# A single-core transformer pair of blocks: the opening's loads, squares and VectorE order rewritten, and TensorE's order in the banded attention

## What is computed

```python
h = _rmsnorm(x, norm_mix_g)
proj = h @ w_in                                   # short conv, long conv, queries, gates
memn = _rmsnorm(mem, norm_mem_g)
k, vm = jnp.split(memn @ w_kv, 2, axis=-1)        # 256 memory positions
...
merged = g[:, :, 0] * y_a + g[:, :, 1] * y_b + g[:, :, 2] * y_c
x = x + merged @ w_o
x = x + _conv_ffn(x, norm_ffn_g, w_up, conv_ffn_w, w_down)
...
q, k, v, z = jnp.split(xn @ w_in, [nq, nq + nkv, nq + 2 * nkv], axis=-1)
o = banded_attention(q, k, v, t5_table, SWA_WINDOW, sinks)
x = x + (o * jax.nn.silu(z)) @ w_out              # then a last RMS norm
```

## Time and profile before

| | before |
|---|---|
| median of 3 runs | 1213.76 us (1213.65 to 1213.79) |
| the profiled execution, its time | 1213.99 us |
| its span | 1212.2 us |
| granted TensorE clock, mean | 0.999 |
| PE busy | 1203.6 us, 99% |
| PE weight loads | 994.2 us, 82% |
| DVE busy | 827.7 us, 68% |
| ACT busy | 490.6 us, 40% |
| DMA over the span | 105 GB/s |

### The profile page before, as it was taken

How to read it: one execution, slowest core, us unless ns; L and a number is a source line. 1 busy time by engine, 2 the same in 40 slices (tenths; PEclk the granted TensorE clock), 3 DMA queues, 4 the chain that set the end, 5 groups by cost and what they waited for, 6 DMA issues and landing times.

```text
span 1212.2 us, 15930 instructions
## 1 busy us (share of the span) xinstructions
PE 1203.6 (99%) x5656; PEld 994.2 (82%) x5656; DVE 827.7 (68%) x1293; ACT 490.6 (40%) x785; POOL 7.5 (1%) x18
## 2 busy tenths in 40 slices
PE   9999999999999999999999999999999999999998
PEld 8788888888888888888888888888888888887786
DVE  6858897797789987554357866566654444578762
ACT  7543323332333323552334534334333333155643
POOL 0000000000000000000000000000000000000000
PEclk9999999999999999999999999999999999999999
DMA  8533232222222332243322232233233534221221
GB/s 325 175 104 104 87 104 73 84 87 86 71 87 87 104 105 87 87 174 104 104 78 97 87 106 90 98 104 104 87 110 104 174 104 139 87 71 53 74 66 70
DMA packets 35842, 125.51 MB, mean 104 GB/s; under 512 B 4081, under 2 KB 5761, under 8 KB 35537
## 3 DMA queue, kind: packets, MB, share of 16 engines
q1 hardware_dynamic: 33424, 116.41, 28.8%
q0 software_dynamic: 928, 6.08, 1.4%
q10 hardware_dynamic: 1440, 2.36, 0.5%
HBM read 122.72 MB, written 4.21 MB: 105 GB/s over the span
## 4 chain that ended last, share of the span: by engine, by line
PE 95%; DVE 2%; DMA 1%; ACT 0%; issue 0%; SPq 0%; DVEq 0%; ACTq 0%
PE acc L852 80%; PE acc L869 5%; PE side L1189 2%; PE acc L1189 2%; DMA w_raw<-weights 1%; PE side L1115 1%; PE acc L1153 1%; DVE w_low L1223 1%; PE acc L886 1%; PE side L991 1%; PE side L1011 1%; PE acc L1125 1%; DVE part L1260 0%; PE side L1001 0%; DVE part L1351 0%
## 5 line engine op out<-in xcount | busy, mean ns | idle before, releaser
L852 PE MATMUL acc<-h_high,w_high 128*128 128x512 f32 x880 | 343.2, 390 | 0.0
L852 PE MATMUL acc<-h_low,w_high 128*128 128x512 f32 x880 | 342.7, 389 | 0.0
L852 PE MATMUL acc<-h_high,w_low 128*128 128x512 f32 x880 | 342.7, 389 | 0.0
L1223 DVE TENSOR_TENSOR w_low<-w_raw,w_high 128x1024 fp32r<-128x1024 f32 x213 | 257.6, 1221 | 42.0 <-ACT w_high L474 38.8
L474 ACT ACTIVATE w_high<-w_raw 128x1024 fp32r<-128x1024 f32 x213 | 221.0, 1051 | 103.2 <-PE acc L852 86.9
L852 PEld LDWEIGHTS acc<-h_high,w_low 128*128 128x128 f32 x880 | 165.2, 188 | 34.3
L852 PEld LDWEIGHTS acc<-h_high,w_high 128*128 128x128 f32 x880 | 165.2, 188 | 34.3 <-DVE w_low L1223 0.2
L852 PEld LDWEIGHTS acc<-h_low,w_high 128*128 128x128 f32 x880 | 165.3, 188 | 33.9
L1298 DVE SCALAR_TENSOR_TENSOR convs<-long_u,par,convs 128x510 f32<-128x510 f32 (+28 forms) x232 | 170.3, 734 | 6.6
L852 PE MATMUL acc<-f_high,w_high 128*128 128x512 f32 x176 | 68.6, 390 | 0.0
L852 PE MATMUL acc<-f_low,w_high 128*128 128x512 f32 x176 | 68.5, 389 | 0.0
(11 more groups left out here) (331 smaller groups left out, 1815.5 us busy)
## 6 DMA issues: line engine op xcount, KB each, us to landing
w_raw<-weights SPq DMA_DIRECT2D x213, 512.0 KB, 3.3
x_in<-x SPq DMA_DIRECT2D x4, 512.0 KB, 10.1
x<-x POOLq DMA_DIRECT2D x1, 2048.0 KB, 8.7
rows_dram<-strip_dram POOLq DMA_DIRECT2D x1, 2048.0 KB, 11.3
w_raw<-weights SPq DMA_DIRECT2D x4, 384.0 KB, 7.0
mem_in<-mem ACTq DMA_DIRECT2D x4, 256.0 KB, 7.1
bias<-rows_dram POOLq DMA_DIRECT2D x1, 1024.0 KB, 7.1
out<-result ACTq DMA_DIRECT2D x4, 256.0 KB, 2.6
```

Source lines behind the costliest of these rows:

```text
L852: mm = pe.matmul(acc[:, bank, 0:width], w[:, s, (skip + b) * P:(skip + b + 1) * P], moving[v][:, k, :], start=first and b == 0 and w is w_ ...
L1223: dve.tensor_tensor(w_low[:, s, :], raw[s][:, :], w_high[:, s, :].bitcast(F32), ALU.subtract)\
```

## The change

**Loads of the opening.** The first piece of unit 0 and tile 0 of the memory are transfers of their own (128 KB each, semaphores `alone_landed` and `mem_alone_landed`), and the first piece of units 1 and 2 follows as a transfer of 256 KB. The memory's tile 1 is loaded by ACT, tiles 2 and 3 by the software queue of GpSimd (POOL), tiles 4 to 7 by SP. The parameters (`par`, 254 KB) move from ACT's queue to the end of SP's opening. ACT issues two transfers instead of six. Units 4 and 5 are loaded at once into two spare buffers (`w_spare`), ahead of x; `raw_of` picks them.

**Order of the pieces.** ACT and DVE do unit 0's piece, then the two tiles of the memory, then the pieces of units 1 and 2. PE takes a unit's two tiles before the next unit's, and waits for that unit's piece alone. The zero products are three instead of four. DVE waits for the gains before its first instruction.

**Squares.** One `tensor_reduce` sums the memory's eight tiles (2048 elements a partition), one more those of x (4096 elements), both reading along k with n outside, so that neighbours in the sum lie 1 KB and 2 KB apart. They replace three additions of 128x512 and one of 128x256, and seven of 128x512.

**Order of DVE, ACT and PE** between unit 3 and unit 17: as in the diff; `total(N_X)` moves behind `value_slab(0, 0)`, `spread(N_X)` behind `value_slab(0, 1)`, tiles 5, 6 and 7 of x behind unit 17.

**Banded attention.** `outputs(j)` no longer follows `product` of its own iteration, but the two turns of the next one.

```diff
@@ sync
-            for c in range(CHUNKS):
+            def first_piece(c, u):
                 at = c * CHUNK
+            sp.dma_start(w_raw[:, 0, 0:CHUNK], weights[0, :, 0:CHUNK]).then_inc(alone_landed, 16)
+            sp.dma_start(mem_in[:, 0, :], mem[:, 0, :]).then_inc(mem_alone_landed, 16)
+            first_piece(0, 1)
+            first_piece(1, 0)
+            first_piece(2, 0)
+            load_memory(2)
+            first_piece(3, 0)
+            load_memory(3)
             for s in range(EARLY, SLOTS):
                 sp.dma_start(raw[s][:, :], weights[s]).then_inc(landed[s], 16)
+            for s in range(SPARE):
+                sp.dma_start(w_spare[:, s, :], weights[SLOTS + s]).then_inc(landed[s], 16)
...
             load_x(0)
             load_x(1)
-            load(1, 0)
-            load(1, 1)
+            load(1, 2)
+            load(1, 3)
             load_x(2)
-            load(1, 2)
             load_x(3)
-            load(1, 3)
+            sp.dma_start(par[:, KT:N_PARAMS], params[:, KT:N_PARAMS]).then_inc(par_landed, 16)
@@ gpsimd
             pool.memset(conv_sum, 0.0).then_inc(zeros_set, 1)
+            pool.dma_start(mem_in[:, 2:4, :], mem[:, 2:4, :]).then_inc(mem_landed[1], 16)
             pool.dma_start(ones, consts[:, 0:P]).then_inc(consts_landed, 16)
@@ scalar
             act.dma_start(par[:, 0:KT], params[:, 0:KT]).then_inc(gain_landed, 16)
-            for c in range(1, CHUNKS):
-                load_memory(c)
-            act.dma_start(par[:, KT:N_PARAMS], params[:, KT:N_PARAMS]).then_inc(par_landed, 16)
+            act.dma_start(mem_in[:, 1, :], mem[:, 1, :]).then_inc(mem_landed[0], 16)
...
+            unit_high(11, 12)
             for k in range(2):
                 x_high(k)
-            unit_high(12, 13)
-            for k in range(2, 5):
-                x_high(k)
+            unit_high(13)
+            x_high(2)
+            unit_high(14)
+            x_high(3)
+            unit_high(15)
+            take_values(0)
+            x_high(4)
+            unit_high(16, 17)
+            for k in range(5, KT):
                 x_high(k)
@@ tensor
-            for width in (SEQ, SEQ, SEQ, MEM):
+            for width in (SEQ, SEQ, MEM):
                 pe.matmul(side[:, 3, 0:width], conv_sum[:, 0:P], conv_sum[:, 0:width], start=True, stop=True)
...
-            total(N_X, SEQ)
             spread(N_MEM, MEM)
             value_slab(0, 0)
+            total(N_X, SEQ)
+            value_slab(0, 1)
             spread(N_X, SEQ)
...
                 for step in (2 * j, 2 * j + 1):
                     turn(step)
+                if j:
+                    outputs(j - 1)
...
-                outputs(j)
+            outputs(KT - 1)
@@ vector
+            def add_mem_squares():
+                dve.wait_ge(mem_squared, CHUNKS)
+                dve.tensor_reduce(sum_sq[:, 0:MEM], mem_sq.rearrange("p k n -> p n k"), AX_X, ALU.add)\
                    .then_inc(mem_added, 1)
...
+            def add_x_squares():
+                dve.wait_ge(x_squared, KT)
+                dve.tensor_reduce(x_sum, x_sq.rearrange("p k n -> p n k"), AX_X, ALU.add).then_inc(x_added, 1)
+
+            unit_low(3, 4, 5)
+            add_mem_squares()
+            unit_low(6, 7)
             mean_square(N_MEM, MEM)
-            add_x_squares(5, 6, 7)
-            unit_low(8, 9)
-            mean_square(N_X, SEQ)
-            dve.wait_ge(par_landed, 16)
+            unit_low(8)
+            add_x_squares()
+            unit_low(9)
             dve.wait_ge(rstd_ready, 1)
             dve.tensor_copy(rstd_mem, side[:, 2, 0:MEM]).then_inc(rstd_mem_kept, 1)
             dve.wait_ge(rstd_mem_kept, 1)
-            take_k(0, 4, 1, 5)
-            unit_low(10, 11)
+            take_k(2, 6)
+            unit_low(10)
+            mean_square(N_X, SEQ)
+            take_k(3, 7, 0, 4, 1, 5)
+            unit_low(11, 12)
+            dve.wait_ge(par_landed, 16)
             dve.wait_ge(rstd_ready, 2)
             x_tiles(0, 1)
-            take_k(2, 6, 3, 7)
+            unit_low(13)
             x_tiles(2)
-            unit_low(12, 13)
-            x_tiles(3, 4, 5)
-            unit_low(14, 15)
-            x_tiles(6)
+            unit_low(14)
+            x_tiles(3)
+            unit_low(15)
+            x_tiles(4)
             unit_low(16, 17)
-            x_tiles(7)
+            x_tiles(5, 6, 7)
             low_tile(KT, KT - 1, h_high, h_low, SEQ)
```

More of the change, by code:

```diff
@@ L64 @@
 EARLY = 3
+SPARE = 2
 CHUNK = UNIT // CHUNKS
@@ L380, in build, with raw_of @@
         GATE_TILES = {2 * KT - 2: (0, 1), 2 * KT - 1: (2, 3)}
+        def raw_of(m, s):
+            return w_spare[:, s, :] if isinstance(m, int) and m == 1 and s < SPARE else raw[s][:, :]
         def last_bank(t, half):
@@ L505, in x_high @@
                 act.activation(h_high[:, k, :], part[:, k % 2, :], ACT.Copy).then_inc(act_high, 1)
-            def load_memory(c):
-                act.dma_start(mem_in[:, 2 * c:2 * c + 2, :], mem[:, 2 * c:2 * c + 2, :]).then_inc(mem_landed[c], 16)
-            load_memory(0)
             act.dma_start(par[:, 0:KT], params[:, 0:KT]).then_inc(gain_landed, 16)
-            for c in range(1, CHUNKS):
-                load_memory(c)
-            act.dma_start(par[:, KT:N_PARAMS], params[:, KT:N_PARAMS]).then_inc(par_landed, 16)
+            act.dma_start(mem_in[:, 1, :], mem[:, 1, :]).then_inc(mem_landed[0], 16)
             for c in range(CHUNKS):
-                act.wait_ge(first_landed[c], 16)
                 for s in range(EARLY):
                     at = c * CHUNK
+                    if c == 0 and s == 0:
+                        act.wait_ge(alone_landed, 16)
+                    else:
+                        act.wait_ge(first_landed[c], 16)
                     act.activation(w_high[:, s, at:at + CHUNK], raw[s][:, at:at + CHUNK], ACT.Copy)\
                        .then_inc(chunk_high if c < CHUNKS - 1 else weight_high, 1)
[L521 to L526, removed]
+                    if s == 0:
+                        act.wait_ge(gain_landed, 16)
+                        for k in range(2 * c, 2 * c + 2):
+                            if k == 0:
+                                act.wait_ge(mem_alone_landed, 16)
+                            else:
+                                act.wait_ge(mem_landed[c], 16)
+                            act.activation(mem_high[:, k, :], mem_in[:, k, :], ACT.Copy, scale=col("g_mem", k))\
+                               .then_inc(act_high, 1)
             def unit_high(*units):
@@ L948, in _ @@
             pe.wait_ge(zeros_set, 1)
-            for width in (SEQ, SEQ, SEQ, MEM):
+            for width in (SEQ, SEQ, MEM):
                 pe.matmul(side[:, 3, 0:width], conv_sum[:, 0:P], conv_sum[:, 0:width], start=True, stop=True)
[L951 to L957, removed]
-                for i in range(EARLY):
-                    key_part(i, k)
+            for c in range(CHUNKS):
+                for i in range(EARLY):
+                    if c < CHUNKS - 1:
+                        pe.wait_ge(chunk_low, EARLY * c + i + 1)
+                    else:
+                        pe.wait_ge(weight_low, i + 1)
+                    for k in range(2 * c, 2 * c + 2):
+                        pe.wait_ge(act_low, k + 1)
+                        key_part(i, k)
             for i in range(EARLY, 6):
@@ L965, in _ @@
             key_unit(7)
-            total(N_X, SEQ)
             spread(N_MEM, MEM)
             value_slab(0, 0)
+            total(N_X, SEQ)
+            value_slab(0, 1)
             spread(N_X, SEQ)
-            for i in range(1, SLOTS):
+            for i in range(2, SLOTS):
                 value_slab(0, i)
@@ L1314, in _ @@
                        .then_inc(chunk_low if c < CHUNKS - 1 else weight_low, 1)
[L1315 to L1320, removed]
+                    for k in range(2 * c, 2 * c + 2) if s == 0 else ():
+                        dve.wait_ge(act_high, k + 1)
+                        dve.scalar_tensor_tensor(mem_low[:, k, :], mem_in[:, k, :], col("g_mem", k),
+                                                 mem_high[:, k, :].bitcast(F32), ALU.mult, ALU.subtract)\
+                           .then_inc(act_low, 1)
             def unit_low(*units):
```

62 lines of the change are left out of this document (19 added, 43 removed).

## The result

The changed kernel takes 1218.31 us (median of 6 runs, 1217.90 to 1219.81) against 1213.77 for the kernel before (6 runs): a ratio of 1.0038, 95% interval 1.0028 to 1.0047. It is slower by 4.5 us. The forecast was 1212.8, with a range of 1210.2 to 1217.6. The profiled execution took 1218.23 with a span of 1216.5, which is 4.3 more than the span before.

What follows compares the result with a forecast made beforehand. PE bounds the kernel (busy 99%), with DVE setting the opening. Opening 0.0 and attention -0.95 take the profiled 1213.99 to 1213.0; the median lies 0.2 below: 1212.8 us, range 1210.2 to 1217.6.

Steps and rivals of the forecast that it cites:

- What bounds the opening: Opening: DVE's list sets when PE starts on x, 55.95 us before; forecast 55.9, so 0.0 gained.
- The sum of x: DVE in the opening: one reduce over x's 4096 elements takes 4.4 us, the memory's 2048 take 2.3.
- rival A: Strided sums on DVE run at half rate, x's 8.7 us: 1217.5 us; decides once x's sum takes over 7.8; chance 0.3.
- The other end of the bounds: DVE's strided sums with each element at the price of two: 8.7 us for x, 4.4 for the memory.
- When the sum can start: Opening: DVE can sum x's squares at 26.8 us, after 8.26 MB of loads and ACT's rounding of unit 8 and last squares.
- DVE's list and the four waits: From the end of x's sum to PE's start on x: 20.2 us of DVE work, 4.2 of waits for ACT, 0.25 to start.
- First pieces: Start of the opening: PE's first product at 5.9 us, 2.1 earlier; POOL's pair at 8.3 costs 1.7; all inside DVE's time.
- rival C: Opening: POOL's memory tiles land at 10 to 11 us, shifting DVE's list by 1 to 2.4: 1214 to 1215.2 us; chance 0.08.
- The attention: Banded attention: the new order saves PE 0.16 us an iteration at its seams, 0.95 over six, bounds 0.0 and 2.1.
- outputs to scores: Attention seam on PE, half the columns to half the rows: between 0 and 0.20 us, taken as 0.20.
- next to nothing left: Attention: turns wanted 1.9 us earlier; the second turn's row is ready in time, with almost no margin.
- B: Opening: the DVE and ACT ping-pong does not bind, PE does, reaching x at 53.6: 1210.4 us; chance 0.17.

Runs made afterwards that it cites:

- e3: The change with each strided reduce (x's and the memory's squares) replaced by three additions of neighbouring elements, in the same place of DVE's list: 1215.29 us.
- e4: The change with ACT rounding units 13 to 16 one step earlier, DVE's list as in the change: 1215.90 us.
- e6: The change with the edits of both e3 and e4: 1211.75 us, ratio 0.9983 to the kernel before.
- e5: The change with ACT writing the squares of x so that the eight elements of one sum are neighbours for the one reduce: 1217.22 us.
- e8: The change with five extra unread reduces on DVE at distances of 4, 8 and 16 bytes, only their lengths counting: 1229.08 us, one run.
- e7: e6 with the memory's second pair of tiles moved from POOL's to SP's queue and the late parameters from SP's to ACT's: 1211.25 us.
- e2: The change with the attention's old order, so its opening alone: 1219.01 us.
- e10: e7 with the first pieces of units 0, 1 and 2 as one transfer of 384 KB again: 1211.42 us.

## Why the prediction was wrong, by its own steps

- **What bounds the opening** was right: DVE's list up to units 16 and 17. e3, e4 and e6 shorten that list, and PE follows.
- **The sum of x** is the step that failed most: the length taken for one reduce over distant elements. "I take 4.4, from the nearest row" measured 7.43: 3.0 us. The nearest row was a reduce of neighbours, and the distance, which I named in rival A, is what makes the price: e5 has 4.42 with the distance gone. The memory's was 3.94, not 2.3, and cost nothing that shows. The other end of the bounds, 8.7, was nearer. The rule on SBUF's lines in the Trainium skill ("Advanced Engine Details and Errata", section "SBUF Cachelines") was right against my choice, and e8 agrees with its two hits on a line: 1.21 us with 8 bytes between the elements, 1.93 with 16.
- **When the sum can start.** Forecast 26.8, measured 28.63: 1.8 us. The unit was to be seen by ACT at 24.65 and was at 26.40. The DMA did move 405 GB/s, but by 26.2 us it had moved 8.88 MB, not the 8.26 that I counted up to unit 8: part of what stands behind in the queue is moved before unit 8 is complete. The 0.62 MB are 1.5 us, and 3.20 instead of 3.30 MB in the first 12 us are 0.25. No run moves unit 8 alone in the change; that these 1.8 us reach PE is read from the chain.
- **DVE's list and the four waits** were right: forecast 20.2 + 4.2 + 0.25 = 24.65, measured 35.98 to 60.83, 24.85. The waits were 0.92 to 1.05, as forecast. So 3.0 + 1.8 + 0.2 = 5.0 are the 4.9 by which PE's start on x missed the 55.9.
- **First pieces.** PE's first product was forecast at 5.9; it came at 5.66. POOL's pair landed 4.6 us from its issue, which began at 1.28, so near 6 and not at 8.3, and rival C, its lateness, had the wrong sign: it came early, and ACT waited 1.63 us for the piece of units 1 and 2, a wait that is 0.19 in e7, where that pair stands behind the piece in SP's queue. That stayed hidden, as said.
- **The attention**: each seam came as forecast, outputs to scores at about 0.2 in its two parts among them, so the half-columns to half-rows switch pays like the others. The gain was 0.63 by the trace and 0.56 by the runs, not 0.95. Some 0.2 of it is one iteration where the second turn comes late: DVE's row for it ends at 1114.49, and PE's turn starts at 1114.55, 0.60 behind the first and not 0.43. That was the "next to nothing left". At the starts of the products of z, PE lags behind the kernel before by 4.88, 4.73, 4.57, 4.63, 4.48, 4.33 and 4.22 us, and by 4.25 at the end. So four of the six seams gave 0.15 or 0.16, the late one lost 0.06, the last gave 0.11, and 0.03 were lost behind it.
- **The rivals and the range.** A gave 1217.5 for sums at half rate. It was the right case, with a sum that was shorter (7.43, under the 7.8 that I had as its turning point) and a start that was later; that its time came within 0.8 us is in part luck, since these two errors have opposite signs. I had bounded the sum, and not the start of it, so the range ended 0.7 too low. By its own turning point, the sum alone would have left the time inside 0.2%; it took the late start as well. B, PE bounding the opening, needed both costs gone: e6 and e7 are B, at 1211.75 and 1211.25 against the 1210.4 that I gave it.

## What to carry to other kernels

Before one long instruction takes the place of several, look at the distance between the elements it reads: here eight float32 tiles were summed faster by three wide additions that read neighbouring elements (4.2 us) than by one reduce across the tiles (7.43), and laying the data otherwise only moved the price to the engine that writes. Where two engines hand tiles to each other in turn, let the one that feeds round one unit ahead: a different order on ACT alone was worth 2.4 to 3.1 us. An earlier first tile is worth only what the second tile can follow.

## What the runs showed of the hardware

**Distance in SBUF.** Both DVE and ACT keep their pace of neighbours at 8 bytes from element to element and lose it at 16: 1.21 against 1.93 us for a reduce of 1024, 0.42 against 0.65 for 256 on ACT. At 12 bytes DVE lies between, at 1.51; there a line of 16 bytes, by the rule cited above, serves sometimes two elements and sometimes one. "SBUF — State Buffer" of the Trainium skill, section "Door 1: The DMA port swizzle", has float32 free up to a distance of four elements. These runs show it free up to two. For the whole sum of x the price is 1.81 ns an element at 2 KB and 1.08 at 4 bytes.

**The clock after a wait.** In some executions the waits in the opening are followed by a lower granted clock. The stretches of e3's profile (us, busy of PE, PEld, DVE, ACT, POOL, granted clock, DMA share, GB/s):

```profile
55.00:60.00 5.00, 3.16 (x10) 2.25 (x9) 4.91 (x6) 2.11 (x4) 0.00 (x0) 0.78 0.57 166
60.00:65.00 5.00, 5.00 (x20) 4.04 (x20) 2.10 (x4) 4.22 (x7) 0.00 (x0) 0.88 0.21 82
```

PE's timeline of the same run, at its start on x:

```profile
57.65 0.61 PE L895 MATMUL acc<-h_high,w_high 128*128 128x512 f32 x1 [1.84 <-DVE w_low L1253]
58.07 0.63 PE L895 MATMUL acc<-h_low,w_high 128*128 128x512 f32 x1
58.49 0.63 PE L895 MATMUL acc<-h_high,w_low 128*128 128x512 f32 x1
```

Behind an idle time of 1.84 us the products stand 0.42 apart, where 0.23 is usual. The two stretches miss 0.22 and 0.12 of 5 us, 1.7 us of full clock, which at the lower of the two levels (1.2 of 2.4 GHz) is 3.4 us spent there; the 48 products of the first pair take 12.77 us in it and 11.14 in the change. This execution's span is 1214.9, and the shortest of the same kernel 1213.0. e2 shows the same behind its wait for x's sum (0.76 and 0.89 between 35 and 45 us), and e8 reads 0.52 and 0.50 from 40 to 50 us, where PE waits 9.0. But the profiled run of the change itself has 1.00 in every stretch, so such a wait doesn't always bring it. A fallen clock would explain that the medians of e3 and e4 lie above their forecasts and their lowest runs do not: of e4's 11 runs the four longest (1216.07 to 1218.18) have a mean granted clock of 0.996 or 0.997, the other seven 0.998 or 0.999. The prediction gave the waits of PE no such price. It isn't the whole of the spread: the runs of e7 lie within 0.5 us of each other, those of the change within 1.9 and of e4 within 3.4, but e6 spreads by 1.0, not the 0.6 expected of it, and e10 by 2.2, with no wait of PE behind its first product. What decides in which run the clock falls stays open.
